# Two-block network on one core: order of norm sums, waits of the projections, layer norm's tiles, and the end in halves

## The reference, cut to what matters

```python
h = concatenate([meta, first_block(x, ...)], axis=1)
h = h + 0.5 * swiglu_ffn(rmsnorm(h, ffn1_norm), ffn1_w_gu, ffn1_w_down)
h = h + token_mixer(rmsnorm(h, mix_norm), ...)
h = h + 0.5 * swiglu_ffn(rmsnorm(h, ffn2_norm), ffn2_w_gu, ffn2_w_down)
return rmsnorm(h, final_norm)[:, N_META:, :]

def token_mixer(h, ...):
    x_rnn, y_rnn, glu_v, glu_g, gate_a, gate_b = split(h @ w_in + b_in)
    y_a = (rg_lru(conv4(x_rnn)) * gelu(y_rnn)) @ rnn_w_proj
    v = silu(layernorm(conv31(glu_v * sigmoid(glu_g)), ln_g, ln_b))
    y_b = v @ conv_w_proj + conv_b_proj
    return (sigmoid(gate_a) * y_a + sigmoid(gate_b) * y_b) @ w_out
```

## Time and profile before

| | |
|---|---|
| median of 3 runs | 2611.89 us |
| the profiled execution's own time | 2606.13 us |
| its span, first to last instruction | 2604.4 us |
| mean granted TensorE clock | 0.986 |
| TensorE busy | 2505.3 us |
| VectorE busy | 1625.9 us (62%) |
| ScalarE busy | 1002.4 us (38%) |

### The profile page before, as it was taken

One profiled execution on the slowest core, in us unless ns is written; L12 is line 12 of the kernel. 1 busy time (PEld: TensorE's weight loads), 2 busy tenths in 40 slices (PEclk: granted clock), 3 DMA queues, 4 the chain that ended last, 5 costly groups with the idle time before them and its releaser, 6 DMA issues.

```text
span 2604.4 us, 40290 instructions
## 1 busy us (share of the span) xinstructions
PE 2505.3 (96%) x14488; PEld 2165.1 (83%) x14488; DVE 1625.9 (62%) x2396; ACT 1002.4 (38%) x1358; POOL 113.7 (4%) x139
## 2 busy tenths in 40 slices
PE   7999999999999998999999999989999999999996
PEld 3888888888888875888789999979988778888885
DVE  6577777777777665444555343468999975544445
ACT  4344443444444323333335222235455543322222
POOL 0011111121112000000000000000000000000000
PEclk9999999999999998999999999989999999999998
DMA  6212221221122222222222222222222222222222
GB/s 240 73 60 78 72 65 63 72 80 65 64 66 71 97 92 70 73 72 72 74 89 89 89 89 92 92 82 94 94 88 97 90 79 97 90 96 97 90 95 89
DMA packets 59835, 223.99 MB, mean 86 GB/s; under 512 B 6496, under 2 KB 6496, under 8 KB 59264
## 3 DMA queue, kind: packets, MB, share of 16 engines
q1 hardware_dynamic: 56688, 208.99, 24.1%
q0 software_dynamic: 3088, 14.29, 1.6%
HBM read 221.15 MB, written 2.10 MB: 86 GB/s over the span
## 4 chain that ended last, share of the span: by engine, by line
PE 86%; DVE 5%; ACT 4%; issue 3%; DMA 1%; DVEq 0%; ACTq 0%; SPq 0%; POOL 0%
PE ps L465 76%; PE ps L630 4%; PE ps L652 1%; PE ps L522 1%; DVE w_lo L1454 1%; ACT L1060 1%; PE ps L643 1%; DMA ada_raw<-in_ada_weights_dram 1%; PE ps L671 1%; ACT w_hi L937 1%; PE ps L662 1%; PE ps L617 1%; PE ps L664 1%; PE ps L663 1%; DVE n_tmp L1478 0%
## 5 line engine op out<-in xcount | busy, mean ns | idle before, releaser
L937 ACT ACTIVATE w_hi<-w_raw 128x1024 fp32r<-128x1024 f32 (+1 forms) x360 | 378.1, 1050 | 1002.6 <-PE ps L465 992.1
L1454 DVE TENSOR_TENSOR w_lo<-w_raw,w_hi 128x1024 fp32r<-128x1024 f32 (+1 forms) x360 | 434.9, 1208 | 247.6 <-ACT w_hi L937 237.8
L465 PE MATMUL ps<-n_hi,w_hi 128*128 128x512 f32 (+1 forms) x992 | 323.4, 358 | 17.8 <-DVE n_lo L1481 8.0
L465 PE MATMUL ps<-n_lo,w_hi 128*128 128x512 f32 (+1 forms) x992 | 320.6, 355 | 0.0
L465 PE MATMUL ps<-n_hi,w_lo 128*128 128x512 f32 (+1 forms) x992 | 320.0, 354 | 0.0
L465 PE MATMUL ps<-h_hi,w_hi 128*128 128x512 f32 x640 | 271.6, 424 | 5.3 <-DVE h_lo L1586 3.1
L465 PE MATMUL ps<-h_hi,w_lo 128*128 128x512 f32 x640 | 253.9, 397 | 0.0
L465 PE MATMUL ps<-h_lo,w_hi 128*128 128x512 f32 x640 | 253.3, 396 | 0.0
L465 PEld LDWEIGHTS ps<-n_hi,w_hi 128*128 128x128 f32 x992 | 175.8, 191 | 49.9 <-issue 9.8
L465 PEld LDWEIGHTS ps<-n_lo,w_hi 128*128 128x128 f32 x992 | 176.6, 191 | 27.2 <-issue 0.2
L465 PEld LDWEIGHTS ps<-n_hi,w_lo 128*128 128x128 f32 x992 | 176.0, 191 | 26.7
(11 more groups left out here) (352 smaller groups left out, 5046.1 us busy)
## 6 DMA issues: line engine op xcount, KB each, us to landing
w_raw<-in_weights_dram SPq DMA_DIRECT2D x376, 512.0 KB, 3.3
ada_raw<-in_ada_weights_dram SPq DMA_DIRECT2D x4, 2048.0 KB, 20.9
gate_raw<-in_gate_weights_dram POOLq DMA_DIRECT2D x16, 512.0 KB, 3.6
x<-in_x_dram SPq DMA_DIRECT2D x1, 2048.0 KB, 12.8
x<-in_x_dram POOLq DMA_DIRECT2D x1, 2048.0 KB, 8.0
out_dram<-fin POOLq DMA_DIRECT2D x1, 2048.0 KB, 6.5
xc<-in_ctx_dram SPq DMA_DIRECT2D x1, 1024.0 KB, 19.4
masks<-in_masks_dram POOLq DMA_DIRECT2D x1, 512.0 KB, 5.2
```

Source lines behind the costliest of these rows:

```text
L465: last = nc.tensor.matmul(o, w, xp, start=start and n == 0, stop=stop and n == 2)
L937: run(w_hi[:, s, 0:n], w_raw[:, s, 0:n], ACT.Copy).then_inc(hi_ready[s], 1)
L1454: tt(w_lo[:, s, 0:n], w_raw[:, s, 0:n], w_hi[:, s, 0:n].bitcast(F32), ALU.subtract).then_inc(lo_ready[s], 1)
```

## The change

1. In `residual` with sums, VectorE adds the square of the row before ahead of the row's own update, and ScalarE squares a row before it cuts the next weight. The last turn of a loop with a norm behind is written out, and `close_sums` stands between the last update and the last cut.
2. `rnn_out` starts when the third turn's steps are done; the tiles 6 and 7 of its first row wait for a_lo of their own row. The second mean of the layer norm goes behind two tiles of row 6. The projection of the layer norm waits for the gates of its own banks only (7, then 8, instead of 10).
3. At the exit VectorE and ScalarE do several tiles of the layer norm ahead of weight cuts and gates, and ScalarE loads the Silu table early (`warm`).
4. The last two rows of f2c are made in halves of 256 tokens: both weights are taken first, then rows 6 and 7 for the first half, then for the second. Sum, mean, root, reciprocal and products follow by halves, and each of 16 products (128 x 256) is stored by itself, issued by SyncE.

The diff's pieces stand in the order of the file: SyncE and GpSimd, TensorE (`last_rows` to the wait of 7), ScalarE (the `residual` with `square_one`, then the exit with the Silu table), VectorE (the `residual` with `add_square`, the exit, the end).

```diff
+            for n in range(2 * KD):
+                half, k = divmod(n, KD)
+                c = slice(half * HALF_T, (half + 1) * HALF_T)
+                sp.wait_ge(NOUT["lo"], n + 1)
+                sp.dma_start(out[:, k, c], fin[:, k, c]).then_inc(out_s, 16)
...
-            pool.wait_ge(NOUT["lo"], KD)
-            pool.dma_start(out, fin[:]).then_inc(out_s, 16)
...
+            def last_rows(R, N, done, h_, n, count):
+                st.enter(0, 2)
+                s = [take(0), take(1)]
+                for half in range(2):
+                    xs = half_of(*h_, half, n)
+                    for a in range(2):
+                        if half == 0:
+                            pe.wait_ge(R["res"], KD - 2 + a + 1)
+                        last = tiles(s[a], [ps[:, 2 * a + half, 0:n // 2]], xs, range(count), True, True)
+                        last.then_inc(w_used[s[a]] if half else done, 1)
+                        if half and a == 0:
+                            mean_of_half(N, n, 0)
...
             def from_scan(k):
-                pe.wait_ge(mx_dve, KD // 2 * 12 + min(k, KD - 1) - (KD - 1))
+                late = k - (KD - 2)
+                pe.wait_ge(mx_dve, (KD // 2 - 1) * 12 if late < 0 else KD // 2 * 12 - 1 + late)
...
-            pe.wait_ge(mx_dve, KD // 2 * 12 - 2)
+            pe.wait_ge(mx_dve, (KD // 2 - 1) * 12)
             rnn_out((0, 1, 2, 3))
             ln_mean(6, 1, centred_sq[:, KD - 1])
             rnn_out((4, 5))
-            ln_mean(7, 2, centred_sq[:, 0])
-            rnn_out((6, 7))
+            rnn_out((6, 7), lambda: ln_mean(7, 2, centred_sq[:, 0]))
-            pe.wait_ge(YA["res"], KD + 2)
+            pe.wait_ge(YA["res"], 7)
...
                     for a in range(2):
                         for q in range(nb):
-                            if ahead or not isinstance(i, int):
-                                after(a * nb + q)
-                        if sums:
-                            square_one(R, i * 2 + (a + done), src(i * 2 + (a + done)), sq, 2)
+                            if sums and q == nb - 1:
+                                square_one(R, i * 2 + (a + done), src(i * 2 + (a + done)), sq, 2)
+                            after(a * nb + q)
...
             run(n2["sq"][:, 0, 0:T], ps[:, 7], ACT.Sqrt, bias=eps[:]).then_inc(ln_act, 1)
+            run(warm[:], zero[:], ACT.Silu)
-            after(0)
             for k in range(KD):
-                if k == 2:
-                    after(1)
+                if k in (1, 5):
+                    after(k // 5)
...
+                        if sums:
+                            add_square(R, m_, *sums)
                         st.wait_done(dve, a * nb + nb - 1)
                         stt(r_, acc, factor(m_), r_, ALU.mult, ALU.add).then_inc(R["res"], 1)
+                        if last and a:
+                            close_sums(R, N, *sums)
                         if cuts:
                             after(a * nb + nb - 1)
-                        if sums:
-                            add_square(R, m_, *sums)
...
-            after(3)
-            gated(3, 3)
             dve.wait_ge(ln_pe, 1)
             for k in range(KD):
                 tt(cv[:, k], cv[:, k], ps[:, 6], ALU.subtract).then_inc(ln_dve, 1)
+                if k == 1:
+                    after(3)
+            gated(3, 3)
...
                 if k == 4:
                     after(0)
-                    gated(0, 4)
...
             tt(total, total, other, ALU.add).then_inc(ln_sum, 1)
+            gated(0, 4)
             after(1)
+            gated(1, 5)
             dve.wait_ge(ln_act, KD + 1)
             own.link(v.reciprocal(lroot, lroot))
-            gated(1, 5)
-            after(0)
-            gated(0, 6)
             for k in range(KD + 1):
-                if k == 3:
+                if k == 2:
+                    after(0)
+                    gated(0, 6)
+                if k == 6:
                     after(1)
                     gated(1, 7)
...
+            row_(0, 0)
+            add_square(RD2, KD - 2, n2["sum"][:, 0, 0:T], n2["sq"][:, 0, 0:T])
+            row_(1, 0)
+            half_sum(RD2, NOUT, T, 0, 0)
+            half_sum(RD2, NOUT, T, 1, 0)
+            row_(0, 1)
+            half_sum(RD2, NOUT, T, 0, 1)
+            half_inverse(NOUT, T, 0)
+            row_(1, 1)
+            finished(0, range(0, 2))
+            half_sum(RD2, NOUT, T, 1, 1)
+            finished(0, range(2, 6))
+            half_inverse(NOUT, T, 1)
+            finished(0, range(6, KD))
+            finished(1, range(KD))
```

More of the change, by code:

```diff
@@ L49 @@
 FF_GROUPS = (8, 8, 6)
+IN_HALVES = ("f2c",)
+LAG = 4
 DW = 31
@@ L186, in program @@
         eps_sq = g.take("eps_sq", [P, 1])
-        unused = g.take("unused", [P, 1])
+        unused, warm = g.take("unused", [P, 1]), g.take("warm", [P, 1])
         ada0 = g.take("ada0", [P, 16, 2])
@@ L880, in rnn_out @@
                     s = take(n)
-                    tiles(s, [ps[:, YA_BANK[k % 4]]], from_scan if k == 0 else whole(a_hi, a_lo), range(KD), True, True
-                          ).then_inc(w_used[s], 1)
+                    o, xs = [ps[:, YA_BANK[k % 4]]], from_scan if k == 0 else whole(a_hi, a_lo)
+                    first = 0
+                    if aside and n == 0:
+                        first = 2
+                        tiles(s, o, xs, range(first), True, False)
+                        aside()
+                    tiles(s, o, xs, range(first, KD), not first, True, first).then_inc(w_used[s], 1)
                 st.leave(1)
@@ L1319, in feed_forward, with half_square, half_root @@
                     final = tag == tags[-1]
-                    residual(last_R if final else RP[tag], KD // 2, 1,
+                    residual(last_R if final else RP[tag], KD // 2 - (tag in half_done), 1,
                              lambda m_: row(hb, m_)[:, c0:TM], n2["sq"][:, 0, 0:n], final,
-                             not (final and last))
+                             not (final and last) or tag in half_done)
+            def half_square(R, n, a, half):
+                c, m_ = n // 2, KD - 2 + a
+                act.wait_ge(R["res"], 2 + m_ + 2 * half + 1)
+                act.wait_ge(R["add"], KD)
+                run((n2["sq"], n2["tmp"])[a][:, 0, half * c:(half + 1) * c],
+                    hb[:, m_, TM - n + half * c:TM - n + (half + 1) * c], ACT.Square).then_inc(R["sq"], 1)
+            def half_root(N, n, half):
+                c = n // 2
+                act.wait_ge(N["mean"], half + 1)
+                run(n2["sq"][:, 0, half * c:(half + 1) * c], ps[:, 6 + half, 0:c], ACT.Sqrt, bias=eps[:]
+                    ).then_inc(N["root"], 1)
             feed_forward(("f1a", "f1b", "f1c"), RD1, TM, False, sg1, hid1, hid1_hi,
@@ L1810, in one @@
                         stt(r_, acc, factor(m_), r_, ALU.mult, ALU.add).then_inc(R["res"], 1)
+                        if last and a:
+                            close_sums(R, N, *sums)
                         if cuts:
                             after(a * nb + nb - 1)
-                        if sums:
-                            add_square(R, m_, *sums)
-                n_loop = trips if ahead else trips - 1
+                closing = bool(sums and N)
+                n_loop = trips - 1 if closing or not ahead else trips
                 with dve.Fori(0, n_loop) as i:
@@ L1820, in residual @@
                 st.leave(n_loop)
-                if not ahead:
+                if n_loop < trips:
                     st.enter(0, 2 * nb)
-                    one(trips - 1, False)
+                    one(trips - 1, ahead, closing)
                     st.leave(1)
-                if sums:
-                    close_sums(R, N, *sums)
             dve.wait_ge(x1_in_s, 16)
```

79 lines of the change are left out of this document (60 added, 19 removed).

## The result

The changed kernel takes 2571.11 us (median of four runs, 2569.15 to 2573.62), the kernel before in the same comparison 2611.51: a ratio of 0.9848 [0.9833, 0.9862]. The change gives 40 us where 12 were forecast. The profiled execution took 2572.69 us, its span is 2571.0, at a mean clock of 0.989. Before, it was 2606.13, 2604.4 and 0.986. So the two traces differ by 33.4 us, and 7 of the 40 lie in which executions were profiled: that of before stands 5.4 under its median, that of after 1.6 over its own.

The account below looks back on a forecast made before the run. TensorE, working in 96% of the span, was taken as the bound, so only its waits and the tail could gain. N1 2.15, NMIX 2.2, exit 6.4, tail 1.6, less 0.2, made 12.1 off 2611.89: 2599.8 us, range 2592 to 2608.

Parts of the forecast that it names:

- N1: At norm N1, sums one row ahead close at 1002.61 instead of 1004.76: gain 2.15 us.
- NMIX: At norm NMIX, the same sums one row ahead close at 1736.59 against 1738.82: gain 2.23 us.
- Lag of the new order: In the loops, splitting a weight after the square makes rows lag: 0.9 us in f2c, 0.2 in f1c.
- (2): Rival in f2c and f1c: VectorE's loop return costs about 1.2 us, in all 7.0 instead of 1.1; 2605.7 us, chance 0.08.
- (5): Rival: every second row of both loops stands 1.3 us and the clock falls each time; 2615 us, chance 0.03.
- Exit: At the mixer's exit, through the layer norm's projection: earlier rnn_out and fewer waits gain 6.4 us; ends 8.3 and 0 to 2.
- the clock of the pair: Layer norm's projection: clock stays up despite six gaps; a rival kept it low, exit gaining nothing, 2606 us, chance 0.15.
- Tail: Last f2c rows to the end, in halves: computing ends 2.3 us later, the store gains it back; net gain 1.6 us.
- The wait: Ahead of f2c's last two rows, TensorE stands 4.2 us for the second weight's split.
- The store: At the end, the last piece of 128 KB lands in 2.6 us, 3.9 off the 6.5 of the 2 MB store.
- rival (4): At the end, the stores run one at a time, 16 x 2.6 = 42 us: 31 us more, 2631 us, chance 0.02.
- The sum: Whole kernel: 2.15 + 2.2 + 6.4 + 1.6 - 0.2 = 12.1 us gained, giving 2599.8 us.

Follow-up runs that it names:

- e1: Kernel before plus one unused one-column tile, so that every later tile moves by 32 bytes: 2596.5 us against 2610.3, ratio 0.9955.
- e2: Changed kernel with the early Silu written into a second column of `unused`, so no tile moves against before: 2585.92 us, ratio 0.9909.
- e7: Kernel before with only the edits from the scan's last turn to the layer norm's end, no tile moved: 2603.1 us against 2609.88, ratio 0.9977.
- e4: Kernel before plus eight one-column memsets on VectorE ahead of the mixer loop, no tile moved: 2600.05 us against 2610.3, ratio 0.9962.
- e3: Kernel before with only the new order of the norm sums on ScalarE and VectorE, no tile moved: 2593.43 us, ratio 0.9939.
- e6: Kernel before plus an unused tile of 96 bytes, so that all later tiles move by 96 bytes: 2599.04 us, ratio 0.9955.
- e10: Changed kernel, second row's weights taken late and f2c's split before its square, plus rows of n and hid 2048 bytes apart: 2557.02 us, ratio 0.9796.

## Why the prediction was wrong

By its steps:

- **N1**: forecast 2.15, measured 2.13. **NMIX**: 2.2, measured 2.85. The mean was quicker as well, so the root started at 1729.60, behind the table load at 1728.20. The load is now what comes last, as the forecast had it next.
- **Lag of the new order**: in f2c 0.9 was forecast. TensorE's only wait for a weight there is 0.52 us at 2526.66, and the loop lies about 1.1 us behind. In f1c 0.2 was forecast; from its memset to the last update it takes 32.95 us instead of 31.67, so it is 1.3, of which 0.1 belongs to the slower matmuls of 264 columns (31.77 in e1, where only the tiles move) and the rest to the order (32.88 in e2, where they don't). Rivals (2) and (5) didn't come at these loops.
- **Exit**: 6.4, measured 6.7 in the changed kernel, 6.3 in e7's trace and 6.8 in its median. The gap at a_lo, the slow stretch behind it (0.53 from 2046.8 to 2050), the small waits in the pair (five for n_lo, 2.8 us together, and one of 0.57 for the second weight; 3.4 us of standing where 4.6 were told) and the clock of the pair came as told.
- **Tail**: 1.6, measured 3.0, and the sum's own terms (3.9 + 0.2 - 2.3) make 1.8. The wait was right, the computing ended 3.1 later and not 2.3. Behind the last product 4.1 were forecast and 6.1 came. The store was mis-sized: 1.9 us a piece instead of 2.6, issued 0.49 apart and in flight together, so that rival (4) is out. The larger miss is a term that the sum didn't have: before, the last 2.35 us of the span lie behind the landing, and with SyncE in GpSimd's place 1.96 of them are gone. By "Anatomy of one DMA" of the Trainium skill's page "DMA: Bandwidth & Descriptors", which measured transfers issued by GpSimd, a piece would take an estimated 2.3 us; the measured 1.9, issued by SyncE, is below that and below my own figure. The Trainium skill's section "Rules for kernel authors" on that page gives 1 MiB or more per transfer for the highest bandwidth, and that is not what this last store needs: the last of 16 pieces of 128 KB lands 2.66 us behind the last product (0.78 + 1.88), the one of 2 MB 6.83 (0.29 + 6.54). No run has one store of 2 MB issued by SyncE, so what pieces and issuer each do to the landing stays open.
- **The sum**: this is the step that failed. It added up the edits at the places where they act and took every other stretch as it was. Two lines of the diff act elsewhere, and no part of the working costs either. The tile `warm` isn't mentioned; it stands among the diff's first lines, and it moves every operand of TensorE but the weights (13.8 us in e1, 14.8 by e2). The last trips of RC and RD1 as straight code were costed as an order of work, not as code (10.3 us in e4, with 15 fewer transfers of code). By the medians the parts make 14.3 for the place of the tiles, 10.3 for that of the code, 6.8 for the exit (e7), 6.6 for the sums (e3) and about 3 for the tail in the changed kernel: 41, against 40 measured. The 6.6 is a difference of two of the others (16.9 - 10.3) and each part is known to a microsecond or two, so that the sum comes out so close is partly luck.

Could it be read ahead? The size couldn't, since no row of before shows another address. That there was something to lose could. A matmul of 512 columns took 0.2327 us where 512 columns at 2.4 GHz are 0.2133, and I used the first figure without asking for the rest. The 3 us stalls stood in the trace too: in the chain that ended last there is a row of its own for one,

```profile
1842.63 2.80 issue
```

and I had read that view for the duration of a matmul only. "Issue" is idle time that no semaphore explains; the rival that belonged here was that moved code changes it, and the 31 transfers of code stood on the page. My range was too narrow for the same reason: it took in the bounds of each known term, and nothing for a term left out.

What stays open: the exact grain of the placement (128 or 256 bytes, and why mg gains nothing in e6 where g gains 4 ns; no run has every row at a multiple of 256); which boundary VectorE's code crosses between one and eight instructions; why a matmul at its best place still takes 226.8 ns; and what moves whole executions of one kernel by 4 to 5 us.

## What to carry to other kernels

Ask of each line of a diff what it moves besides what it does: a tile of 4 bytes re-places all that is allocated behind it, and an unrolled trip re-places all code behind it. When TensorE bounds the kernel, lay the rows of its moving operands a multiple of 256 bytes apart, try their common start in steps of 32 bytes, and compare its start-to-start time with columns over clock; and look for "issue" ahead of the first instruction of a loop's body on an engine that sets the pace, and for transfers of code there. Where two edits meet on one engine, cost their meeting: the square ahead of the split was right for the sum's end and wrong for the weight behind it.

## What the runs showed of the hardware that I had not expected

- A matmul of 512 fp32 columns takes 233.0 to 233.3 ns from start to start when its moving operand begins 32 bytes past a multiple of 64 bytes, and 226.7 to 227.7 when it begins 32 bytes further on, in the built program 128 past a multiple of 256 (g, a, y, mg; hid 226.8 in e10). h comes down only to 229.3 to 229.8, wherever the shift puts it. In a kernel whose TensorE is busy 96% of the time this is 14 to 15 us, and 22 with the rows of n and hid.
- The Trainium skill's page "SBUF — State Buffer", section "Operand start alignment", asks for a start at a multiple of the element's size, calls that a rule of legality and says that its runs timed nothing. The traces here agree that both places work, and add that they differ by 3% in time.
- VectorE stands 2.96 to 3.08 us at each return of a loop of 268 instructions, or not at all, by where the code lies. The step is the same for every kernel with the tiles of before: 10 to 11 us over three returns, of which 9 are the stalls themselves. With the stalls go five packets of code of 8 KB a turn (15 in all), and without them these are missing.
- Stores of 128 KB land 1.9 us after their issue (median of 16), issued 0.49 us apart, so some four of them are in flight together (1.9/0.49). The products that they store take 0.41 us each (4.05/10), so at the end the issuing sets the pace.
- Which engine waits for the last store matters: the span ends 2.35 us behind its landing with GpSimd (DRAIN of 1.94 us) and 0.39 with SyncE (0.01). From the last product to the end it is 9.2 us in all eight kernels in which GpSimd stores and 3.0 in all five in which SyncE does.
